# Norm stage and input projection of a decoder layer joined in one block, with the first tile pair computed between the transposes

## The reference

```
h    = x * rsqrt(mean(x*x) + 1e-6) * g_pre_mix          # (2048, 1024)
proj = h @ w_in                                         # (1024, 3072)
rq, rk, rv, rg, aq, ak, av = split(proj, [256, 256, 512, 512, 512, 512, 512])
# rq, rk, aq, ak are rotated by the positions; rg goes through silu later
# then: retention, dilated attention, w_out, norm, SwiGLU feed-forward, norm
```

## Time and profile before

| | |
|---|---|
| median of 3 runs | 2921.47 us (2918.26 to 2925.28) |
| span of the profiled execution | 2917.3 us |
| busy: TensorE, VectorE, ACT, GpSimd | 2710.4, 1262.4, 759.5, 503.7 us |
| norm stage, from the start to the first weight cast | 57.3 us |
| projection, first product to last | 59.4 to 613.5 us |
| chain that ended last, TensorE lines 1357 and 1375 (feed-forward) | 32% and 16% of the span |
| idle of TensorE before line 372 (projection) | 26.4 us |

### The profile page before, as it was taken

One profiled execution on the slowest core, in us unless ns is written; L12 is line 12 of the kernel. 1 busy time (PEld: TensorE's weight loads), 2 busy tenths in 40 slices (PEclk: granted clock), 3 DMA queues, 4 the chain that ended last, 5 costly groups with the idle time before them and its releaser, 6 DMA issues.

```text
span 2917.3 us, 36840 instructions
## 1 busy us (share of the span) xinstructions
PE 2710.4 (93%) x13096; PEld 2277.9 (78%) x13096; DVE 1262.4 (43%) x2463; ACT 759.5 (26%) x1786; POOL 503.7 (17%) x370
## 2 busy tenths in 40 slices
PE   6999999959999969999599999999999999999995
PEld 4777777749999947777488888888888888888884
DVE  6212455205655667887233333333344333333334
ACT  4112111116766732232211111111121111111111
POOL 2953445100000046666000000000000000000000
PEclk9999999979999979999799999999999999999998
DMA  5222222354424234555631111121153111121103
GB/s 170 69 68 65 79 97 102 114 140 119 125 78 105 89 116 154 178 180 160 217 102 44 58 43 43 43 66 49 53 198 119 49 43 43 43 72 43 43 15 101
DMA packets 219873, 269.65 MB, mean 92 GB/s; under 512 B 12160, under 2 KB 164608, under 8 KB 219008
## 3 DMA queue, kind: packets, MB, share of 16 engines
q1 hardware_dynamic: 219776, 268.42, 29.3%
HBM read 188.29 MB, written 80.08 MB: 92 GB/s over the span
## 4 chain that ended last, share of the span: by engine, by line
PE 48%; DMA 2%; DVE 1%; SPq 0%; issue 0%; ACT 0%; POOL 0%; DVEq 0%; ACTq 0%
PE ff_psum_gu L1357 32%; PE ff_psum_down L1375 16%; DMA out<-ff_x 1%; DMA ff_h_lo<-h_lo 0%; DMA ff_x<-x 0%; SPq L1290 0%; DVE ff_x L1514 0%; DVE ff_total L1511 0%; DVE ff_total L1498 0%; DVE ff_down_lo L1476 0%; DVE ff_w_lo L1470 0%; SPq L1295 0%; DVE ff_gated L1483 0%; SPq L1279 0%; DVE ff_total L1495 0%
## 5 line engine op out<-in xcount | busy, mean ns | idle before, releaser
L1357 PE MATMUL ff_psum_gu<-ff_h_hi,ff_w_hi 128*128 128x512 f32 x1408 | 549.7, 390 | 22.3 <-DMA ff_h_lo<-h_lo 22.3
L1357 PE MATMUL ff_psum_gu<-ff_h_lo,ff_w_hi 128*128 128x512 f32 x1408 | 549.3, 390 | 0.0
L1357 PE MATMUL ff_psum_gu<-ff_h_hi,ff_w_lo 128*128 128x512 f32 x1408 | 549.1, 390 | 0.0
L1483 DVE TENSOR_TENSOR ff_gated<-ff_gated,ff_psum_gu 128x512 f32<-128x512 f32 x88 | 60.5, 688 | 628.2 <-PE ff_psum_gu L1357 628.2
L372 PE MATMUL pr_psum_acc<-hT_hi,pr_w_hi 128*128 128x512 f32 x768 | 303.0, 395 | 26.4 <-DVE pr_w_lo L311 16.1
L1357 PEld LDWEIGHTS ff_psum_gu<-ff_h_hi,ff_w_hi 128*128 128x128 f32 x1408 | 265.3, 188 | 78.1 <-issue 18.7
L1357 PEld LDWEIGHTS ff_psum_gu<-ff_h_hi,ff_w_lo 128*128 128x128 f32 x1408 | 265.2, 188 | 55.2
L1357 PEld LDWEIGHTS ff_psum_gu<-ff_h_lo,ff_w_hi 128*128 128x128 f32 x1408 | 265.4, 188 | 55.0
L372 PE MATMUL pr_psum_acc<-hT_lo,pr_w_hi 128*128 128x512 f32 x768 | 300.3, 391 | 0.0
L372 PE MATMUL pr_psum_acc<-hT_hi,pr_w_lo 128*128 128x512 f32 x768 | 300.3, 391 | 0.0
L1375 PE MATMUL ff_psum_down<-ff_down_hi,ff_a_hi 128*128 128x512 f32 x704 | 274.8, 390 | 14.8 <-DVE ff_total L1498 13.9
(11 more groups left out here) (156 smaller groups left out, 4199.1 us busy)
## 6 DMA issues: line engine op xcount, KB each, us to landing
ff_raw<-in_w_gate SPq DMA_DIRECT2D x22, 1024.0 KB, 5.5
ff_raw<-in_w_up SPq DMA_DIRECT2D x22, 1024.0 KB, 7.9
ff_down_raw<-in_w_down SPq DMA_DIRECT2D x22, 1024.0 KB, 4.9
projT<-pr_rows SPq DMA_DIRECT2D x64, 256.0 KB, 2.4
att_out<-at_orow SPq DMA_DIRECT2D x192, 66.0 KB, 1.6
mx_att_in<-att_out SPq DMA_DIRECT2D x16, 792.0 KB, 4.8
w_raw<-in_w_in SPq DMA_DIRECT2D x24, 512.0 KB, 4.3
nt_xin<-in_x SPq DMA_DIRECT2D x16, 512.0 KB, 3.5
```

The lines of the kernel that those rows point to most:

```text
L1357: last = nc.tensor.matmul(gu_ps[:, tile, n], w[:, n, k, cols], h[:, k, t], start=i == 0, stop=i == 3 * KT - 1)
L1483: nc.vector.tensor_tensor(gated[:, tile], gated[:, tile], gu_ps[:, tile, 1], ALU.mult).then_inc(mul_done, 1)
```

## The change

Both stages become one block in `project`; `normed_transpose` goes, and its loops are written out. Pair 0 (the two first value tiles, 8 groups) is no longer part of the loop: TensorE does the transposes of chunks 0 to 3, and then before each half group (12 matmuls) of group g = 0, 1, 2 the transposes of one chunk of the next four; the groups go through both tiles at one g before the next g. The two weight splits of pair 0 stand in VectorE's steps 3 and 5. `acc` has four banks, used in turn, since `tp` takes the other four; so TensorE waits for the copy of four groups back, not eight. `tile_done` goes: the splits wait for `group_done` themselves, and TensorE has no wait between tiles. The squares have one buffer instead of two. The tables' inputs are loaded behind the last transposes, since the tables lie where the norm stage's buffers were. The other sections, the attention, the mixing and the feed-forward stages are as before.

```diff
-    NR = 4
-    C_ADDED = 2
+    NR, NX = 4, 4
+    C_ADDED, C_COPIED = 2, GROUPS
...
-        acc = m.ps("acc", [P, 2, GROUPS, GROUP])
+        acc = m.ps("acc", [P, GROUPS, GROUP])
+        tp = m.ps("tp", [P, 2, KT, P])
-        tile_done = m.sem("tile_done")
...
+        FIRST_PAIR = SECTIONS[0][0]
+        HEAD = 2 * GROUPS
...
+            pos = 1
             for first, n, kind in SECTIONS:
-                yield kind, first, first + n, pos - first
+                at, n = (first + 1, n - 1) if pos == 1 else (first, n)
+                yield kind, at, at + n, pos - at
...
+                def load_x(c):
+                    if c >= NX:
+                        sp.wait_ge(normed, c - NX + 1)
+                    sp.dma_start(xin[:, c % NX, :], D["x"][bass.ts(c, P), :]).then_inc(loaded[c % NX], 16)
...
+                tiles = [2 * pair + s for first, n, _ in SECTIONS for pair in range(first, first + n) for s in range(2)]
+                load_x(0)
+                sp.dma_start(gain[:], D["g_pre_mix"].broadcast_to([P, DM])).then_inc(consts, 16)
+                sp.dma_start(ident[:], D["ident"]).then_inc(consts, 16)
+                load_x(1)
+                load_w(tiles[0] * P)
+                load_x(2)
+                load_x(3)
+                sp.wait_ge(split, 1)
+                load_w(tiles[1] * P)
+                load_x(4)
+                load_x(5)
+                sp.wait_ge(split, 2)
+                load_w(tiles[2] * P)
+                for c in range(6, CHUNKS):
+                    load_x(c)
+                    if c >= 9 and c % 2:
+                        store_head((c - 9) // 2)
+                sp.wait_ge(transposed, CHUNKS)
+                sp.dma_start(rotation[:], D["rotation"]).then_inc(late_consts, 16)
+                    sp.dma_start(table[kind][1][:].bitcast(I32), D["positions"].broadcast_to([P, SEQ])).then_inc(late_consts, 16)
+                for n in range(4, HEAD):
+                    store_head(n)
+                sp.wait_ge(split, 3)
+                load_w(tiles[3] * P)
...
-                dve.sem_inc(tile_done, 2)
-                    dve.wait_ge(tile_done, t + 1)
+                    if not head:
+                        dve.wait_ge(group_done, 8 * pos - 8 + HEAD - 1 + s if isinstance(pos, int) and pos == 1 else 8 * pos - 8 + GROUPS * (s + 1))
...
-                split_tile(0, 0)
-                split_tile(0, 1)
-                dve.wait_ge(consts, 48)
+                dve.wait_ge(consts, 32)
...
+                for c in range(CHUNKS + 2):
+                    step(c)
+                    if c == 3:
+                        split_tile(0, 0, head=True)
+                    if c == 5:
+                        split_tile(0, 1, head=True)
+                split_tile(1, 0)
+                split_tile(1, 1)
...
-                pe.sem_inc(copied, 2 * GROUPS)
-                with pe.Fori(0, pairs) as pos:
+                pe.sem_inc(copied, C_COPIED)
+                pe.wait_ge(consts, 32)
+
+                def transposes(c):
+
+                    pe.wait_ge(normed, c + 1)
+                    if c > 1:
+                        pe.wait_ge(h_lo_done, c - 1)
+                    for k in range(KT):
+                        last = nc.tensor.transpose(tp[:, c % 2, k, :], xn[:, c % 2, k * P:(k + 1) * P], ident[:])
+                    last.then_inc(transposed, 1)
+
+                def product(s, bank, g, ks):
+
+                    t = slice(g * GROUP, (g + 1) * GROUP)
+                    for k in ks:
+                        for n, (w, h) in enumerate(((w_hi, hT_hi), (w_hi, hT_lo), (w_lo, hT_hi))):
+                            last = nc.tensor.matmul(acc[:, bank, :], w[:, s, k, :], h[:, k, t],
+                                                    start=k == 0 and n == 0, stop=k == KT - 1 and n == 2)
+                    return last
+
+                for c in range(GROUPS):
+                    transposes(c)
+                for g in range(GROUPS):
+                    for q in range(4):
+                        s, half, n = q // 2, q % 2, 2 * g + q // 2
+                        if g + 1 < GROUPS:
+                            transposes(4 * (g + 1) + q)
+                        if half == 0:
+                            pe.wait_ge(split, s + 1)
+                            pe.wait_ge(h_hi_done, 4 * g + 4)
+                            pe.wait_ge(h_lo_done, 4 * g + 4)
+                            pe.wait_ge(copied, n + 1)
+                        last = product(s, n % GROUPS, g, range(half * KT // 2, (half + 1) * KT // 2))
+                        if half == 1:
+                            last.then_inc(group_done, 1)
+
+                with pe.Fori(1, pairs) as pos:
                     for s in range(2):
                         pe.wait_ge(split, 2 * pos + s + 1)
                         for g in range(GROUPS):
                             pe.wait_ge(copied, 8 * pos + s * GROUPS + g + 1)
-                            t = slice(g * GROUP, (g + 1) * GROUP)
-                            n = 0
-                            for k in range(KT):
-                                for w, h in ((w_hi, hT_hi), (w_hi, hT_lo), (w_lo, hT_hi)):
-                                    last = nc.tensor.matmul(acc[:, s, g, :], w[:, s, k, :], h[:, k, t],
-                                                            start=n == 0, stop=n == 3 * KT - 1)
-                                    n += 1
-                            last.then_inc(group_done, 1)
-                        pe.wait_ge(group_done, 8 * pos + (s + 1) * GROUPS)
-                        pe.sem_inc(tile_done, 1)
+                            product(s, g, g, range(KT)).then_inc(group_done, 1)
...
+
+                def copy_head(n):
+
+                    act.wait_ge(row_free[n % NR], 16 * (n // NR) + 16)
+                    act.wait_ge(group_done, n + 1)
+                    nc.scalar.activation(rows[:, n % NR, :], acc[:, n % GROUPS, :], ACT.Copy).then_inc(copied, 1)
+                for c in range(CHUNKS + 2):
+                    if c < CHUNKS:
+                        x = c % NX
+                        act.wait_ge(loaded[x], 16 * (c // NX) + 16)
+                        if c >= NX:
+                            act.wait_ge(meaned, c - NX + 1)
+                        if c:
+                            act.wait_ge(summed, c)
+                        nc.scalar.activation(squares[:], xin[:, x, :], ACT.Square, accum_out=sumsq[:, x:x + 1]).then_inc(summed, 1)
+                    if c >= 2:
+                        act.wait_ge(transposed, c - 1)
+                        nc.scalar.activation(hT_hi[:, :, bass.ts(c - 2, P)], tp[:, c % 2], ACT.Copy).then_inc(h_hi_done, 1)
+                    if c >= 8 and c % 2 == 0:
+                        copy_head((c - 8) // 2)
+                for n in range((CHUNKS + 1 - 8) // 2 + 1, HEAD):
+                    copy_head(n)
+
...
-                            nc.scalar.activation(rows[:, i % NR, :], acc[:, i // GROUPS, i % GROUPS, :],
+                            nc.scalar.activation(rows[:, i % NR, :], acc[:, i % GROUPS, :],
...
-                pool.wait_ge(consts, 48)
+                pool.wait_ge(late_consts, 48)
...
-        keep = {n: ctx.enter_context(nc.sbuf_tensor(n, [P, KT, SEQ], F32R)) for n in ("hT_hi", "hT_lo")}
-        keep["w_raw"] = ctx.enter_context(nc.sbuf_tensor("w_raw", [P, KT, P], F32))
-        normed_transpose(nc, D, keep)
-        project(nc, D, keep)
+    project(nc, D)
```

More of the change, by code:

```diff
@@ L55, in sems @@
         return [self.sem(f"{name}{i}") for i in range(n)]
[L58 to L156, removed]
-                        before = (x - 1) % NX
-                        nc.vector.scalar_tensor_tensor(xn[:, 1 - s, :], xin[:, before, :], rstd[:, before:before + 1], gain[:],
-                                                       ALU.mult, ALU.mult).then_inc(normed, 1)
-                    if has(c, 0):
-                        dve.wait_ge(summed, c + 1)
-                        nc.vector.tensor_scalar(meansq[:, x:x + 1], sumsq[:, x:x + 1], 1.0 / DM, RMS_EPS,
-                                                ALU.mult, ALU.add).then_inc(meaned, 1)
-                    if has(c, 2):
-                        dve.wait_ge(hi_done, c - 1)
-                        nc.vector.tensor_tensor(hT_lo[:, :, bass.ts(c - 2, P)], tp[:, s],
-                                                hT_hi[:, :, bass.ts(c - 2, P)].bitcast(F32),
-                                                ALU.subtract).then_inc(lo_done, 1)
-                steps(dve, step, 2)
-            @block.tensor
[L173 to L180, removed]
-                        for k in range(KT):
-                            last = nc.tensor.transpose(tp[:, 1 - s, k, :], xn[:, 1 - s, k * P:(k + 1) * P], ident[:])
-                        last.then_inc(transposed, 1)
-                steps(pe, step, 1)
@@ L220, in project @@
         rows = m.sb("rows", [P, NR, GROUP])
+        rotation = m.sb("rotation", [P, 4])
+        quarter = m.sb("quarter", [P, 1])
```

(13 more changed lines are left out.)

61 lines of the change are left out of this document (47 added, 14 removed).

## The result

The changed kernel takes **2900.1 us** (median of 4 runs, 2899.69 to 2902.28); the kernel before took 2921.65 us (median of 4, 2918.26 to 2925.28). The ratio is 0.9927, with a 95% interval of 0.9913 to 0.9941: 21.6 us less, where the forecast was 22.2. The profiled span is 2900.1 us against 2917.3, only 17.2 less. A span is about 2 us shorter than the time of its run, and the two profiled executions lie at opposite ends: the old one near the lower end of its runs, the new one at the upper (its run took 2902.28).

| | before | after | gained so far |
|---|---|---|---|
| pair 1 starts | 106.5 | 90.8 | 15.7 |
| pair 6 starts | 332.7 | 313.9 | 18.8 |
| projection ends | 613.5 | 594.8 | 18.7 |
| mixing stage starts | 1050.2 | 1031.6 | 18.6 |
| end | 2917.3 | 2900.1 | 17.2 |

What follows compares the result with a forecast made beforehand. The change is worth what it takes out of TensorE's path before the attention stage. Gains 12.2 + 8.6 + 1.4 = 22.2 take the span from 2917.3 to 2895.1; plus 4.2 gives 2899.3 us, range 2890 to 2910.

Steps and rivals of the forecast that it cites:

- Part A: Head: pair 0 moves in among the norm stage's transposes; head ends at 94.4 instead of 106.55, gaining 12.2 us.
- two gates on SP: Head: SP holds weight tiles and x chunks 4 and 6 behind two splits; chunk 6 transposed at 44.6, not about 27.
- 1.8 later is 18.4: Head: first weight split starts 1.8 us after chunk 1's low half, for the 2.0 us weight load, and ends at 20.4.
- the 89.4: Head's early bound: no slow stretch, loads 0.8 us sooner at both gates, 2.7 us a half; a gain of 17.
- Part B: Tile changes of pairs 1 to 5: without TensorE's self-wait and the tile_done increment, 8.6 us gained, at least 4.3.
- 40 groups at 5.44 are 217.6: Pairs 1 to 5: 226.2 us before, less 40 groups at the old pace, leaves the gain of 8.6 us.
- Part C: Attention-part pairs 6 to 9: nothing gained, since weight casts 25.3 us apart wait for late loads; banks covered by 4.7 us.
- Part D: After the chain, from 546.27 us on: two tile boundaries lose their idle and drain, 1.4 us gained.
- Tables: GpSimd's tables, asked for behind the last transposes, run from 88 to 209; ACT wants them at 225, 16 us of cover.
- The ramp: Rival: each gated load in the head costs 4 us more, head ends at 102.4, time 2907; chance 0.11.
- The four banks: Rival: copies lag 5 us more and TensorE stops in each late tile, time 2905; chance 0.04.
- Half the clock: Rival: transposes keep TensorE at 1.2 GHz through the head, 7.1 us a chunk, time 2941; chance 0.07.

Runs made afterwards that it cites:

- x_loads_ahead: The changed kernel with x chunks 4 and 5 asked for before SP's first wait for a weight split, 6 to 8 before the second: 2892.87 us, ratio 0.9900.
- weights_asked_early: small_tiles_behind with SP's split wait and next weight load ahead of a tile's four row stores, not behind them: 2876.40 us, ratio 0.9838.
- small_tiles_behind: The changed kernel with five small norm-stage tiles made behind the row buffers, so the weights lie where they did before: 2893.57 us, ratio 0.9903.
- all_three: The changed kernel with small tiles behind, weights asked for early and x loads ahead together: 2867.39 us, ratio 0.9810.
- before_weights_moved_640: The kernel before with 640 unused bytes ahead of w_raw, so w_hi lies at 152320 as in the changed kernel: 2928.82 us in one run.

## Why the prediction was right, and where its errors met

The time came out as forecast, but not the sum. Its parts as measured, by the starts of the pairs: A 15.7 (forecast 12.2), B 3.1 (8.6), the attention pairs 1.0 (0), the last two pairs -1.1 (1.4), together 18.7 instead of 22.2, and the span 2900.1 instead of 2895.1. The 4.2 us that I put between span and median were in part those of one old execution near the low end; the new span equals the new median, since its execution was the slowest of four. So the terms missed by +3.5, -5.5, +1.0 and -2.5, and which executions were profiled made up the rest. That the total fits to 0.8 us is luck: the interval of the ratio is 17 to 25 us of gain. What the gain consists of was forecast rightly all the same: the head and the drain, with nothing from the pairs that wait for late weight loads.

**Part A, too small by 3.5.** The structure held: two gates on SP, six chunks and one group before the dense part, then TensorE as the bound. Chunk 7 onwards came every 3.65 us (forecast 3.7), with 8 transposes in 1.04. What failed is the step "1.8 later is 18.4, and the first weight split [...] ends at 20.4" (the 1.8 stands for the 2.0 worked out just before): the weight tile ahead of chunks 2 and 3 held nothing up that the split waits for. The low half of chunk 1 ended at 16.5 as before, and the split at 17.14 + 1.23 = 18.4, 2.0 earlier. The loads behind each gate landed after 4.8 and 4.9 us, not 5.7, in a queue that was otherwise empty. These three make 3.7 of the 4.4 by which chunk 6 was earlier (40.2 against 44.6). Some came back: the slow stretch made the step from chunk 6 to 7 6.54 us instead of 3.65, so 2.9, where I had added 1.7. The cause of the ramp is shown by x_loads_ahead. One bound was worked out wrong: with its own terms the 89.4 should be some 88.5, which changes nothing in the range.

**Part B, the right mechanism and a missing term.** The drain stood at the boundaries, and nothing else in pairs 1 to 5: that step is shown twice, by its removal and by its return. What failed is "40 groups at 5.44 are 217.6", which took a group's pace for a property of its instructions. Five pairs took 223.1 us, since a group takes 5.577: 0.137 x 40 = 5.5 us, the whole miss. That the place of the weights costs this is shown by moving them in either kernel with no other edit.

**Part C, nearly nothing gained, for the reason given.** The chain of casts over late loads set the pace of pairs 8 to 10; the slower matmuls took up part of the waiting time there (split waits 8.4 us after, 11.2 before without the 4.9 at the seam). weights_asked_early shows the cause: the load asked for before the stores, and every one of these waits is gone. The banks were covered, as forecast.

**Part D** lost 1.1 instead of gaining 1.4. Pairs 10 and 11 took 92.6 us before, 93.7 after and 90.7 in small_tiles_behind: with the weights in their old place they gain 2.0, and the new place costs 3.0, the same missing term.

**Tables**: they ran from 86.30 to 207.9, one microsecond before the forecast's 209, and ACT used them at 225.36. Cover 17.5 us (forecast 16).

```profile
86.30 2.91 POOL L436 CAST pr_cos_ret<-pr_sin_ret 128x2048 f32<-128x2048 int32 x1
...
205.97 1.90 POOL L445 TENSOR_SCALAR pr_cos_att<-pr_cos_att 128x2048 f32<-128x2048 f32 x1
```

**Rivals.** The ramp was better, not worse. The four banks never bound. Half the clock held up to 32.7 us, as the starts of the matmuls show, and then for one stretch of 6.8 us around an idle of 2.64, but not under steady work: from 50 to 90 us the granted clock is 1.00 with nearly a third of the matmuls transposes. The 1.97 us of a chunk is the half level and the 1.04 the full one: after chunk 4 and after chunk 6 the products too are 0.43 apart, beside the others 0.23. Transposes alone never had the full level: in the kernel before all 16 chunks, from 9.7 to 54.5 us with waits between, took 1.94 to 1.97 each, and the first matmuls at full pace came at 63.4, 4 us into the products. The Trainium skill ("TensorE: Matmul & The Clock Gate", Part 4, PE-mode transpose) says that full clock does not engage for transposes; the norm stage of the kernel before agrees with it, the 1.04 of the transposes between products does not.

## What to carry to other kernels

When stages are merged or tiles declared in another order, compute where stationary and moving operands come to lie, and compare the spacing of the matmuls before and after: here it cost 6 to 7 us of a change that gained 22, with not one instruction of the projection's loop different. In a queue in program order, put no request that could go at once behind a wait that belongs to another; two gains found here (7 and 17 us) are only that. And a forecast should be checked by the boundaries of its stages: a total that fits to 0.8 us hid errors of 2.5 to 5.5.

## What the runs showed of the hardware beyond that

The spacing of the projection's matmuls (128 x 128 stationary, 512 columns, rounded float32 parts) depends on the distance of the two operands in SBUF: 226.7 to 227.0 ns at a multiple of 256 bytes (three layouts), 232.4 to 232.7 at 128 and 640, 233.3 at 32 and 64. Other shapes were not tried, and why it is so was not tested. The rest of this kernel fits: the feed-forward stage, whose operands lie a multiple of 256 apart, runs at 226.7, and the products of the mixing stage, at a distance of 96 past one by the sizes of its tiles, at some 234, which the forecast had taken for the pace of a mix with transposes. Neither was moved to see.

The length of the attention stage, in which no instruction was changed, was 415.8 us before, 417.1 after and 420.1 in small_tiles_behind. It is tempting to say that it gives part of a gain back, but the 14 traces do not bear that out: all lie between 415.8 and 420.1, 419.2 where it starts 54 us earlier (all_three) and 419.3 where it starts 6.5 us later (before_weights_moved_640). There is one trace of each kernel, so what in it varies stays open; it is a reason not to read single microseconds out of two spans.
